# mLSTM walked in 128-token tiles instead of 64-token chunks, with the next head's projections behind the numerators

## What is computed

```python
CHUNK = 64
b = jnp.cumsum(log_f.reshape(B, H, N, CHUNK), axis=-1)
d_log = jnp.where(mask, b[..., :, None] - b[..., None, :] + i_pre[..., None, :], -jnp.inf)
a = b_last[..., None] - b + i_pre
kv_loc = jnp.einsum("bhncd,bhnce->bhnde", k * jnp.exp(a - m_loc[..., None])[..., None], v)
...
C_new = s_old[..., None, None] * C + s_loc[..., None, None] * kv_loc
...
s = jnp.einsum("bhncd,bhnsd->bhncs", q, k) * jnp.exp(d_log - m_i[..., None])
num = jnp.einsum("bhncs,bhnse->bhnce", s, v) + e_inter[..., None] * jnp.einsum("bhncd,bhnde->bhnce", q, C_s)
den = jnp.sum(s, -1) + e_inter * jnp.einsum("bhncd,bhnd->bhnc", q, n_s)
h = num / jnp.maximum(jnp.abs(den), jnp.exp(-m_i))[..., None]
```

## Time and profile before

| | us |
|---|---|
| median of 3 runs | 1222.42 |
| lowest and highest of them | 1221.04, 1225.42 |
| profiled execution, first to last instruction (its own time as the trace gives it) | 1221.9 |
| TensorE busy | 1113.7 |
| VectorE busy | 566.8 |
| ScalarE busy | 308.1 |
| GpSimd busy | 95.8 |

### The profile page before, as it was taken

How to read it: one execution, slowest core, us unless ns; L and a number is a source line. 1 busy time by engine, 2 the same in 40 slices (tenths; PEclk the granted TensorE clock), 3 DMA queues, 4 the chain that set the end, 5 groups by cost and what they waited for, 6 DMA issues and landing times.

```text
span 1221.9 us, 13917 instructions
## 1 busy us (share of the span) xinstructions
PE 1113.7 (91%) x4612; PEld 487.9 (40%) x4642; DVE 566.8 (46%) x1301; ACT 308.1 (25%) x553; POOL 95.8 (8%) x163
## 2 busy tenths in 40 slices
PE   5999999989689999999959999999968999999984
PEld 0444534435343333333335545544543333333332
DVE  0363231327654555555564131333774455555545
ACT  0533320402231211121233232341232121222213
POOL 4000000003320000000040000000430000000000
PEclk9999999999789999999979999999879999999998
DMA  9867448445799999999751312212559899999952
GB/s 375 363 250 301 181 181 314 188 187 207 281 373 349 394 390 405 401 398 399 271 207 34 121 69 104 77 40 108 202 196 376 342 396 397 398 385 384 405 211 87
DMA packets 51241, 328.33 MB, mean 269 GB/s; under 512 B 6144, under 2 KB 8784, under 8 KB 14464
## 3 DMA queue, kind: packets, MB, share of 16 engines
q1 hardware_dynamic: 44672, 299.92, 61.9%
q0 software_dynamic: 4912, 20.95, 4.5%
q10 hardware_dynamic: 1616, 6.93, 1.5%
HBM read 320.90 MB, written 6.88 MB: 268 GB/s over the span
## 4 chain that ended last, share of the span: by engine, by line
PE 75%; DMA 14%; DVE 5%; ACT 3%; issue 2%; SPq 1%; DVEq 0%; POOL 0%; ACTq 0%; PEldq 0%
PE bank L687 36%; PE bank L1064 17%; DMA ring<-in_w_moe 8%; PE bank L1081 6%; PE bank L1100 5%; PE bank L1101 3%; PE bank L708 3%; DMA ring<-in_w_mod 2%; DMA region<-h_store,toki 1%; DMA ring<-in_w_out 1%; PE bank L1116 1%; PE bank L1090 1%; DMA ring<-in_w_in 1%; PE bank L1073 1%; PE bank L1136 1%
## 5 line engine op out<-in xcount | busy, mean ns | idle before, releaser
L1064 PE MATMUL bank<-ring,region 128*64 128x512 f32 x976 | 226.0, 597 | 11.3 <-DMA ring<-in_w_moe 5.3
L687 PE MATMUL bank<-ring,hT 128*128 128x512 f32 x384 | 171.6, 599 | 1.7 <-DMA ring<-in_w_in 1.7
L1064 PEld LDWEIGHTS bank<-ring,region 128*64 128x64 f32 x976 | 74.4, 137 | 136.6 <-issue 136.3
L1081 PE MATMUL bank<-ring,region 128*64 128x512 f32 x512 | 116.7, 599 | 0.9 <-ACT region L1598 0.9
L687 PEld LDWEIGHTS bank<-ring,hT 128*128 128x128 f32 x384 | 71.0, 190 | 90.4 <-issue 90.1
L2160 DVE SCALAR_TENSOR_TENSOR region<-bank,region 128x512 f32<-128x512 f32 x60 | 45.0, 751 | 113.3 <-PE bank L1081 113.3
L1608 ACT ACTIVATE region<-region 128x512 bf16<-128x512 f32 x60 | 37.8, 630 | 235.7 <-DVE region L2161 235.7
L687 PE MATMUL bank<-ring,region 128*128 128x512 f32 x192 | 86.4, 600 | 5.6 <-DMA ring<-in_w_out 2.1
L687 PE MATMUL bank<-hT,ring 128*128 128x384 f32 x256 | 87.5, 493 | 1.5 <-DMA ring<-in_w_in 1.5
L1100 PE MATMUL bank<-region 128*128 128x512 bf16 x330 | 81.0, 379 | 6.6 <-issue 4.4
L708 PE MATMUL bank<-ring,scT 128*32 128x512 f32 x384 | 55.9, 712 | 15.7 <-DMA ring<-in_w_mod 15.7
(11 more groups left out here) (321 smaller groups left out, 1235.2 us busy)
## 6 DMA issues: line engine op xcount, KB each, us to landing
ring<-in_w_moe SPq DMA_DIRECT2D x195, 1024.0 KB, 8.9
ring<-in_w_mod SPq DMA_DIRECT2D x48, 1024.0 KB, 9.8
ring<-in_w_in SPq DMA_DIRECT2D x24, 1024.0 KB, 7.4
ring<-in_w_out SPq DMA_DIRECT2D x4, 1024.0 KB, 7.4
ring<-in_w_out SPq DMA_DIRECT2D x8, 512.0 KB, 7.8
region<-gate_store POOLq DMA_DIRECT2D x4, 1024.0 KB, 6.4
region<-in_lnrows POOLq DMA_DIRECT2D x4, 1024.0 KB, 8.9
h_store<-region ACTq DMA_DIRECT2D x6, 512.0 KB, 3.0
```

The source lines that it names most:

```text
L687: ins = pe.matmul(out, lhsT, rhs, start=start, stop=stop, skip_group_check=True)
L1064: ins = pe.matmul(bank[6][u * CAP:(u + 1) * CAP, :], xs[:, k, u * CAP:(u + 1) * CAP], places[u][:, at:at + 2 * DE], start=k == 0, stop=k = ...
L1081: ins = pe.matmul(bank[6 + y][u * CAP:(u + 1) * CAP, :], turned[:, f, u * CAP:(u + 1) * CAP], w, start=f == 0, stop=f == FE - 1, skip_grou ...
```

## The change

Layer 1 gets a chain of its own, `CHAIN_ML`, in 128-token tiles: two latent tiles and one context tile for each direction. A head has 4 outer products and 4 updates where it had 10 of each, and 4 `inter` products over full tiles where it had 10 over halves. The context needs no `inter` product any more, and `qe` is made for the latent tokens alone. TensorE does these twelve or so products in one run with nothing between them, raises `num_ready`, and then does the next head's k and v projections in one run. ScalarE's gate, `take_sums` and `head_norm` go ahead of its copy of k. In head 3 the eight products of the output projection that lay in the chain are done after it. The rest of layer 1's gate arithmetic follows the new size. GpSimd rewrites `causal` and `keep` to the 128-token form between the layers, while layer 0's experts run, and VectorE waits for that (`wide`) before the running sums.

```diff
-N_STATES = 10
+N_STATES = (10, 4)
+CHAIN_ML = {(1, 0): (1, 2), (1, 1): (2, 1), (0, 0): (0,), (0, 1): (0,)}
...
                     own(pool.memset(wgt, 0.0))
                     for y in range(4):
                         pool.dma_start(wgt[:, :, 32 * y:32 * y + H], A["wgt"][y]).then_inc(S["wgt_in"], 16)
+
+                    own(pool.memset(causal[:, :, :, :], 1.0))
+                    pool.affine_select(out=causal[:, 0], in_=causal[:, 0], compare_op=ALU.is_ge, fill=0.0,
+                                       base=0, pattern=[[0, NT], [1, P]], channel_multiplier=-1).then_inc(S["wide"], 1)
+                    pool.affine_select(out=causal[:, 1], in_=causal[:, 1], compare_op=ALU.is_ge, fill=0.0,
+                                       base=0, pattern=[[0, NT], [-1, P]], channel_multiplier=1).then_inc(S["wide"], 1)
+                    pool.memset(keep[:, CH:N:P], 1.0).then_inc(S["wide"], 1)
                     pool.wait_ge(S["acc_done"], 1)
...
+                def outer(lat):
+
+                    for d in range(2):
+                        n = CHAIN_ML[lat, d][0]
+                        (bk, col), taken_by = places[n_ds[0] - base]
+                        if taken_by is not None:
+                            pe.wait_ge(S["state_ready"], base + taken_by + 1)
+                        mm(bank[bk][:, col:col + DV + 1], ktok[:, d, n, :], vt[:, b, n, :], True, True).then_inc(S["ds_ready"], 1)
+                        n_ds[0] += 1
+
+                def inter(s):
+
+                    for d in range(2):
+                        t = CHAIN_ML[1, d][s]
+                        if s == 1:
+                            pe.wait_ge(S["state_ready"], base + d + 1)
+                        src = st0[:, d * H + h, :] if s == 0 else st[:, 2 + d, 1, :]
+                        left = qe[:, d, t * P:(t + 1) * P]
+                        if t < NT - 1:
+                            den(d, slice(0, P), t, left, src)
+                        ins = main(d, slice(0, P), t, left, src, False)
+                    return ins
+
+                outer(1)
                 pe.wait_ge(S["qe_ready"], h + 1)
...
-                chain(1, h, inter, fill, inter_den).then_inc(S["num_ready"], 1)
-                project(1, h + 1, PJ_HEAD - 1)
+                inter(0)
+                outer(0)
+                inter(1).then_inc(S["num_ready"], 1)
+                for n in range(1, PJ_HEAD):
+                    project(1, h + 1, n)
...
-                pe.wait_ge(S["state_ready"], N_STATES * H * (l + 1))
-                if l == 0:
-                    out_products(0, 0, 1, range(4, 6))
+                pe.wait_ge(S["state_ready"], states_before(l, H))
+                out_products(l, 0, 1, range(4 * (1 - l), 6))
+                if l == 1:
+                    out_products(1, 0, 0, range(4, 6))
...
+                open_gate(1, h)
+                take_sums(h)
+                head_norm(1, h)
                 for n in range(1, PJ_HEAD):
                     if n == 2:
                         row_weights(h + 1)
-                    if n == 3:
-                        open_gate(1, h)
-                    if n == PJ_HEAD - 1:
-                        take_sums(h)
-                        head_norm(1, h)
                     project(1, h + 1, n)
...
                     g2 = graw[0:H].rearrange("p (d y) n -> p d y n", y=2)
+                    dve.wait_ge(S["wide"], 3)
...
-                            ins = dve.tensor_tensor(qe[:, d, :], qT[:, b, :], spread[b][:, d, 1, :], ALU.mult)
+                            ins = dve.tensor_tensor(qe[:, d, N_CTX:N], qT[:, b, N_CTX:N], spread[b][:, d, 1, N_CTX:N], ALU.mult)
                         ins.then_inc(S["qe_ready"], 1)
-                        states(l, h, (0, 1), n_ds, lambda s: None)
+                        states(l, h, n_ds, lambda s: None)
```

More of the change, by code:

```diff
@@ L106, with states_before, chain_steps @@
 EARLY_SUMS, HIDDEN_SUMS, VALUE_SUMS = ((1, 0), (1, 1), (2, 1)), ((2, 0),), ((0, 0), (0, 1))
-N_STATES = 10
+N_STATES = (10, 4)
 FILL = (((), (3,), (5,), (6, 7)), (2, 4))
 CHAIN = {(1, 0): (2, 3, 4, 5), (1, 1): (5, 4, 3, 2), (0, 0): (0, 1), (0, 1): (1, 0)}
-def chain_steps(dirs):
-    out = []
+CHAIN_ML = {(1, 0): (1, 2), (1, 1): (2, 1), (0, 0): (0,), (0, 1): (0,)}
+def states_before(l, h):
+    return N_STATES[0] * H * l + N_STATES[l] * h
+def chain_steps(l):
+    chain, out = (CHAIN, CHAIN_ML)[l], []
     for s in range(4):
-        for lat, d in CHAIN:
-            if d in dirs and s < len(CHAIN[lat, d]):
-                out.append((lat, d, s, CHAIN[lat, d][s], (not lat) or s < 3))
+        for lat, d in chain:
+            if s < len(chain[lat, d]):
+                out.append((lat, d, s, chain[lat, d][s], (not lat) or s < len(chain[lat, d]) - 1))
     return out
@@ L129, in state_places @@
     past, out = {}, []
-    for lat, d, s, n, more in chain_steps((0, 1)):
+    for lat, d, s, n, more in chain_steps(l):
         if more:
-            key = (6 + n % 2, 0)
+            key = (6 + (n % 2, d)[l], 0)
             out.append((key, past.get(key)))
@@ L826, in attend_gla @@
                     pe.wait_ge(S["pj_free"], n_pj[0])
-                chain(0, h, inter, fill, None).then_inc(S["num_ready"], 1)
+                chain(h, inter, fill).then_inc(S["num_ready"], 1)
                 project(0, h + 1, PJ_HEAD - 1)
@@ L890, in fill @@
-                def fill(s):
-                    for i in FILL[0][s]:
-                        project_half(1, h + 1, i)
-                chain(1, h, inter, fill, inter_den).then_inc(S["num_ready"], 1)
-                project(1, h + 1, PJ_HEAD - 1)
-            def chain(l, h, inter, fill, den):
+                places = state_places(1)
+                base = states_before(1, h)
+                def outer(lat):
[6 more added lines that the diff above has]
+                        n_ds[0] += 1
@@ L922, in chain @@
                                     pe.wait_ge(S["state_ready"], made[lat, d, s - 1])
[L923 to L928, removed]
+                            for d, n, more in here:
+                                ins = inter(d, n, st0[:, d * H + h, :] if s == 0 else st[:, 2 * lat + d, s % 2, :])
                         make = [(d, n) for d, n, more in here if more]
@@ L1743, in keep_hat, with states @@
                 ins.then_inc(S["ht_d"], 1)
-            def states(l, h, dirs, n_ds, between):
+            def states(l, h, n_ds, between):
                 step = 0
-                for lat, d, s, n, more in chain_steps(dirs):
+                for lat, d, s, n, more in chain_steps(l):
                     if not more:
@@ L1757, in states @@
                     dve.wait_ge(S["ds_ready"], i + 1)
-                    last = not lat and s == 1
+                    last = not lat and s == 1 - l
                     w = DV + l
@@ L1970, in between @@
                                 scale_gla(h + 1, (0,))
-                        states(l, h, (0, 1), n_ds, between)
+                        states(l, h, n_ds, between)
                         dve.sem_inc(S["fin_state"], 1)
```

79 lines of the change are left out of this document (37 added, 42 removed).

## The result

The change made the kernel faster: 1207.8 us (median of 4 runs, 1206.1 to 1209.7) against 1222.8 before (1221.0 to 1225.4), a ratio of 0.989 with a 95% interval of 0.987 to 0.991. The forecast was 1207.1, a gain of 15.3 us; the medians of the first measurement differ by 15.0, the profiled spans by 14.0.

A forecast was written before the change was run, and what follows sets the result against it. TensorE, which never runs dry in the heads, was taken as the bound. Savings of 11.2 us in heads 0 to 2 and 4.06 in head 3 made 15.3, so 1222.4 - 15.3 = 1207.1 us; forecast 1204 to 1210, range 1203 to 1214.

The forecast's parts named there:

- The bound: Layer 1's heads: TensorE never runs dry, busy 44.01 of head 1's 44.32 us, so only its own work counts.
- The chain and the projections: Heads 0 to 2: chain 3.90 us plus projections 25.85 make 29.75 instead of 33.49, saving 3.74 a head.
- The 0.98 us: Heads 0 to 2: cost per head of cutting projections into pieces around 64-row and 64-column products, expected to go.
- if the cutting cost stayed: Heads 0 to 2, a case: the projections' cutting cost remains, and the saving is 0.98 us less for each head.
- Packing: Chain: half-array pairs take 0.64 us, less than twice 0.433 for a full product; already counted in the sum.
- the Trainium skill's rule: Half-array products up to twice as fast: nine pairs 3.9 us against 3.5 for eight full products, ending at about 1216.8.
- Waits costed at nothing: Bare chain and k copy: waits stay covered, spare 0.9 and 1.3 us for VectorE, 4.4 us for ScalarE.
- ScalarE's queue: Rival, three heads: sums and norm hold the copy of k past 12.06 us, TensorE stands, 1227 us; 3%.
- Head 3: Chain and output projection's 20 products: 3.90 + 20 x 0.864 = 21.18 us instead of 25.24, saving 4.06.
- Head 0: First head of layer 1: saves 3.74 us like heads 1 and 2, falling from 42.40 to about 38.7 us.
- the 15 that the forecast had named as its sign: Expert stage after the heads: it should begin 15 us earlier, or the forecast is wrong.
- no wait for ScalarE's L1381 or L1384 copies: Sign on TensorE in the heads: no waits for these ScalarE copies should show after the change.

The follow-up runs named there:

- triple: Changed kernel with each latent outer product done three times over in place of once; 1212.1 us, ratio 0.994.
- cut: Changed kernel with four halves of the next head's projections back between the chain's steps, sums and norm later on ScalarE; 1204.4 us, ratio 0.986.
- chunks_bare: Kernel before, 64-token chunks kept, nothing between the chain's steps, projections behind the numerators, ScalarE's order as in the change; 1236.0 us, ratio 1.011.
- best: `k_first` plus, in head 3, an earlier copy-out of head 2's output and a later wait for the last update; 1201.5 us, then 1201.4.
- c_after: The changed kernel run again without edit, for comparison; 1206.9 us, ratio 0.987.
- again_after: The changed kernel once more without edit, beside `k_first` and `best` on one chip; 1206.4 us, ratio 0.990.
- no_masks: Changed kernel without GpSimd's rewriting of the masks and the wait for it, which altered token routing; 1218.6 us.
- old_act: Changed kernel with ScalarE's gate, sums and norm back in their order from before; 1206.1 us, ratio 0.9885.
- k_first: Changed kernel with, in head 0 only, the next head's k projection ahead of the masked products; 1199.7 us, ratio 0.982, then 1201.8, 0.985.

## Why the prediction was right, and where it was off

**The bound.** Right: the sum of TensorE's work sets the heads' time. `triple` puts products in and each costs its full 0.435.

**The chain and the projections.** Right to a tenth: 4.00 us for the chain (3.90), 25.76 for the projections (25.85), 3.81 saved in heads 1 and 2 (3.74). The price of a full product was right (0.435 for 0.433). The 0.98 us were right as a sum. The forecast laid them to cutting projections "around 64-row and 64-column products" and left open whether they would stay; `cut` shows that with full tiles between the pieces they are gone, so its "if the cutting cost stayed" did not come true, with the projections cut or whole.

**Packing.** The forecast went by the rows of the trace, 0.64 us for a pair and 0.433 for a full product, and these held. The half-array pairs gave about half of what a free second product would, and then took 0.98 us a head from their full-size neighbours. By the Trainium skill's rule (TensorEngine Tiling (Array Packing), section Overview) taken at its most, the forecast had the end at 1216.8, which the runs don't bear out. It counted nine pairs there; its own sum for today's chain has ten (five of each kind), and with these the estimate by that rule is about 1215.

**Waits costed at nothing.** Right for VectorE and for ScalarE's queue. VectorE's two updates in head 1 ended at 735.84, and the next products that need them began at 736.16 and, for the second `inter` step, about 737.0. The copy of k begins at 745.20, 7.1 us after the chain's end, and TensorE's next use of its bank is later still. `chunks_bare` shows what such cover is worth: with four latent steps instead of two and no filler, 3.73 us a head.

**Head 3.** 21.74 us from its chain to the turn of its output in place of 25.24: 3.50 saved, 4.06 forecast. The chain took 4.50 us to the first product with `w_out` where 3.90 were put: 4.00 as in the other heads and 0.50 at its end, of which 0.33 is recorded as idle, at the wait for the last state update. The earlier trace rows has the same idle time, 0.30, and the forecast's sum for afterwards left it out. `best`, which moves the wait, has no idle time there and is 0.15 us shorter at that place.

**Head 0.** The term that was mis-sized: 2.25 us saved in the first profile, 3.74 forecast. Its chain and projections behaved like the others'. The wait ahead of the masked products was 2.78 us against 2.62 before, and the products after it took 6.45 instead of 5.13. The forecast took both over unchanged from one profile, and they vary from one execution to the next: from the start of the q projection ahead of it, head 0 ended 2.2, 3.9 and 4.9 us earlier in the three profiles of the changed kernel than in the one of the kernel before (47.66 us).

**How close the number is.** Heads 1 and 2 were right by their mechanism. That the first medians came within 0.3 us of the forecast 15.3 is in part luck: in the profile that the rows are from, head 0 and head 3 fell about 2 us short together and an earlier start of head 0, no part of the forecast, gave 1.25 back; and the later comparisons have 14.9 and 12.6.

**The rest.** The gain went through to the end, as forecast: the experts began 13.97 us earlier, and the span ended 14.0 earlier. That is 1 us less than the 15 that the forecast had named as its sign. Its sign "no wait for ScalarE's L1381 or L1384 copies" overlooked the 0.3 us for the copy of q, which both kernels have.

## What to carry to other kernels

Where one engine never idles, count its instructions' start-to-start times and price the replacement from the nearest rows of full shape; half-array products cost their neighbours something too, which only shows in how much longer the full-size work around them takes (0.98 us a head here). Fillers between dependent steps are worth what the waits they cover are worth: take them away only after following the producer's times through the bare chain, which was free for two latent steps here and 3.7 us a head for four. A wait on TensorE costs more than its length when the granted clock falls after it (by nothing to 3.3 us in the profiles here), so the first place for a spare piece of work is the longest single wait. And a stretch should be compared from profile to profile together with what lies just ahead of it: the changed kernel's head 0 looked 4.3 us shorter in one profile than in another, and 1.7 of that had only moved into the projection in front.

## What the runs showed of the hardware that was not expected

Head 0's wait comes from the rows that ScalarE writes to memory and reads back spread over the partitions. ScalarE waited 4.92 us for that transfer in the first profile, 4.56 in `c_after` and 4.41 in `triple`, and TensorE's opening wait was 2.78, 2.42 and 2.27, shorter by 2.14 each time. What TensorE's twenty records of masked products took behind the wait, in nine profiles, with the granted clock over just these products:

| wait before, us | masked products, us | granted clock | kernel |
|---|---|---|---|
| 1.42, 1.43 | 3.48 | 1.00 | again_after, cut |
| 2.27 | 3.48 | 1.00 | triple |
| 2.29, 2.42 | 5.16, 5.15 | 0.67 | no_masks, c_after |
| 2.52, 2.58 | 6.78, 6.73 | 0.51 | chunks_bare, old_act |
| 2.62 | 5.13 | 0.69 | the kernel before |
| 2.78 | 6.45 | 0.53 | the changed kernel |

Two levels stand behind these means: 1.00 is 2.4 GHz, and the last row is near the lower one, 1.2 GHz. In `k_first`, where TensorE was busy throughout, it was 1.00. Waits that differ by tenths of a microsecond thus went with up to 3.3 us more of TensorE's time. The order of the rows is not strict (2.62 did less than 2.52), and where within the group the clock fell and rose again is not told by the length of the wait alone; what else decides it stays open.

The first row has another cause. In `again_after` and `cut` the clock had fallen already in the q projection ahead of head 0 (6.96 us at 0.75, in place of 5.27 at 1.00), with no idle time of TensorE recorded ahead of it: only the short products of the gates, 2.1 us of them, stood there. ScalarE then waited for q, too, and less of its work was left to wait for in head 0. `best` had the same slow projection. So a fall of the clock in these profiles does not need a wait.
